# Two orders for the first eight chunks of a down projection whose left operand is still being made

## The chip, the cores and the metric

The kernel runs on one core of a Trainium2 chip. The metric is the device time of one execution in microseconds, as the median of three runs. A profile of one further execution, with a time stamp for each instruction, gives the trace.

## The reference

Two transformer blocks on 256 rows of width 2048, in float32. The first has a gated linear attention, then an MLP; the second is a hybrid block. The change concerns the MLP of the first block alone:

```python
def _sq_relu_mlp(h, w_up, w_down):      # w_up 2048 x 8192, w_down 8192 x 2048
    a = jax.nn.relu(h @ w_up)
    return (a * a) @ w_down
# in first_block:
h = h + _sq_relu_mlp(_rmsnorm(h, mlp_norm[i]), mlp_w_up[i], mlp_w_down[i])
```

## The kernel before

**Chunks.** All weight matrices are laid out by the host in one stream of chunks, each 128 x 2048 floats (1 MB): four k tiles of 128 by a column block of 512. SyncE loads them in program order into a ring of four slots (`w_raw`), each when the chunk four before has been used. Each float32 value is split in a high part, rounded to the fp32r format (`w_hi`, ScalarE, L1137), and a low part, the rest (`w_lo`, VectorE, L1810, in the same memory as `w_raw`). TensorE multiplies high by high, low by high and high by low (L585, L586, L587), so a chunk is 4 k tiles x 2 halves of the rows x 3 = 24 matmuls of 512 columns. ScalarE and VectorE work three chunks ahead of TensorE (`AHEAD = 3`). The count `lo_ready` tells TensorE that a chunk is split.

**The MLP.** It runs in four groups (`part` or `g`), each over 2048 of the 8192 hidden columns: 19 chunks of up projection (column blocks 0 to 3; blocks 2 and 3 and some products of sums are formed by `up_pair`) and then 16 chunks of down projection. The down projection sums over k, here the group's 2048 hidden columns, in four quarters q; quarter q is what up block q gave, after relu, square and a transposition. Its column blocks b are those of the result. A down chunk is a pair (b, q). I call the down chunks d0 to d15 in the order in which they come; in the loops over `c` they are c = 19 to 34.

**How a quarter becomes ready.** VectorE or ScalarE takes the up block out of PSUM into `nat`. VectorE transposes it within 32 x 32 squares (`turned`, L2076 for quarters 2 and 3). ScalarE squares it while it moves the squares to their places (`sq`, L1330, sixteen activations in two lots of eight) and rounds it to `a_hi` (L1334). VectorE forms `a_lo` (L2080) and counts `a_low`; TensorE waits for that count before the chunk that uses the quarter first.

**Order on the engines.** Nothing schedules at run time: each engine has one queue, in the order in which the loops write it. In VectorE's loop step c the additions and transpositions stand ahead of `split(c + 3)`. For up block 3 the step is c = 19: the addition L2071 reads its PSUM half and frees it, then comes quarter 2's `a_lo`, then the split of chunk 22.

**PSUM.** The accumulators are two halves, `acc[:, blk % 2]`. Every column block of every product takes the next number `blk`, so a new block needs the half of the block two before, and waits for it in its first matmul:

```python
if first and blk >= 2:
    accs.wait(pe, blk - 2)
```

Down block 0 takes the half of up block 2, down block 1 that of up block 3. The order of the first eight down chunks interleaves two column blocks, and comes from a function:

```python
def LATER(blocks):
    return [(0, 0), (0, 1), (0, 2), (1, 0), (1, 1), (1, 2), (0, 3), (1, 3)] + [(b, q) for b in range(2, blocks) for q in range(4)]
```

Of the kernel before, what the change touches and what calls it, by code (L numbers as in the profile page):

```python
# [17 lines left out]
def build(nc, x, x_turned, mem, mem_turned, stream, cols, rows, wglow, wab, wgu, shapes, masks, out):  # L18
# [27 lines left out]
    with ExitStack() as ctx:  # L46
# [517 lines left out]
        def _(pe):  # L564
            def chunk(c, lhs, k0, blk, first, last, n_k=4, width=N, rows_=(0, 1), done=True, second_half=None):

                if c >= EARLY:
                    pe.wait_ge(lo_ready, ready(c))
                if first and blk >= 2:

                    accs.wait(pe, blk - 2)
                wh = w_hi[:, c % SLOTS].rearrange("p (k n) -> p k n", n=width)
                wl = low_part(c).rearrange("p (k n) -> p k n", n=width)
                for k in range(n_k):
                    if second_half and k == n_k // 2:
                        second_half()
                    if c < EARLY:
                        pe.wait_ge(lo_ready, ready(c, k))
                    if c < NB:
                        pe.wait_ge(x0_low, 4 * c + k + 1)  # L580
                    for m in rows_:
                        xh = lhs[0][:, k0 + k, m * P:(m + 1) * P]
                        xl = lhs[1][:, k0 + k, m * P:(m + 1) * P]
                        dst = acc[:, blk % 2, m, 0:width]
                        pe.matmul(dst, xh, wh[:, k], start=first and k == 0, stop=False)  # L585
                        pe.matmul(dst, xh, wl[:, k], start=False, stop=False)  # L586
                        mm = pe.matmul(dst, xl, wh[:, k], start=False, stop=last and k == n_k - 1)  # L587
                if done:
                    mm.then_inc(used, 1)
                return mm  # L590
# [108 lines left out]
            for c in range(48):  # L699
                b, q = divmod(c, 4)  # L700
# [13 lines left out]
            for c in range(16):  # L714
                b, q = LATER(4)[c]
# [16 lines left out]
            def up_pair(g):  # L732

                c0, left, right = C_MLP + GROUP * g, accs.name["up", g, 2], accs.name["up", g, 3]
                chain, both = tpf(0)[:, 0:N], tpf(0)[:, N:2 * N]

                def of_x(q, m):
                    return [t[:, 4 * q:4 * q + 4, m * P:(m + 1) * P] for t in X]

                def of_s(n):  # L740
                    return s_hi[:, n], s_lo[:, n]

                if g == 0:
                    tps.wait(pe, tps.name["s", 3])
                    tps.wait(pe, tps.name["o", 3])
                else:
                    pe.wait_ge(pair_out, pair_step(g - 1, "p7"))
                product(c0 + 8, *of_x(0, 0), chain, start=True, stop=True)
                chunk(c0 + 9, X, 8, left, True, False)
                if g == 0:  # L750
                    pe.wait_ge(s_formed, 2)
                accs.wait(pe, right - 2)
                product(c0 + 10, *of_s(3), acc[:, right % 2, 0], start=True)
                chunk(c0 + 11, X, 12, left, False, True)
                product(c0 + 12, *of_s(0), both, start=True, stop=True)
                pe.wait_ge(pair_out, pair_step(g, "p1"))
                product(c0 + 13, *of_s(1), chain, stop=True)
                product(c0 + 14, *of_x(1, 0), acc[:, left % 2, 0], stop=True)
                pe.wait_ge(pair_out, pair_step(g, "p6"))
                product(c0 + 15, *of_s(2), chain, stop=True)  # L760
                product(c0 + 16, *of_x(1, 1), acc[:, left % 2, 1], stop=True)
                chunk(c0 + 17, X, 8, right, False, False, rows_=(0,), done=False)
                chunk(c0 + 17, X, 8, right, True, False, rows_=(1,))
                chunk(c0 + 18, X, 12, right, False, True)

            for g in range(GROUPS):
                for c in range(8):
                    b, q = divmod(c, 4)
                    if g == 0 and c < 4:
                        pe.wait_ge(b_low, ROUNDED["norm1", c] + 1)  # L770
                    chunk(C_MLP + GROUP * g + c, X, 4 * q, accs.name["up", g, b], q == 0, q == 3)
                up_pair(g)
                for c in range(16):
                    b, q = LATER(4)[c]
                    if b == 0:
                        pe.wait_ge(a_low, 4 * g + q + 1)
                    chunk(C_MLP + GROUP * g + 19 + c, A, 4 * q, accs.name["down", g, b], q == 0, q == 3)
# [231 lines left out]
            for c in range(50):  # L1009
                if c < 48:  # L1010
                    b, q = divmod(c, 4)
# [8 lines left out]
            for nb in range(NB):  # L1020
                for j in range(16):
                    c = 50 + 16 * nb + j
                    br, q, k0 = BRANCH[j]
# [12 lines left out]
            for c in range(16):  # L1036
                b, q = divmod(c, 4)
# [25 lines left out]
            for c in range(12):  # L1063
                b, q = divmod(c, 4)
# [10 lines left out]
            g = tps.name["xo_"]  # L1075
# [17 lines left out]
            for g in range(2):  # L1093
                for c in range(48):
                    b, q = divmod(c, 4)
                    if c >= 32:
                        b, q = 8 + LATER(4)[c - 32][0], LATER(4)[c - 32][1]
# [699 lines left out]
        def _(dve):  # L1797
# [624 lines left out]
            for nb in range(NB):  # L2422
                for j in range(16):
                    c = 50 + 16 * nb + j
                    br, _, _ = BRANCH[j]
                    if j in (4, 14, 15):

                        gk = 3 * nb + {4: 0, 14: 2, 15: 1}[j]
                        gate, blk = accs.name[("gate", nb, br)], accs.name[("br", nb, br)]
                        dve.wait_ge(used, C_2 + c + 1)  # L2430
                        accs.wait(dve, gate)
                        t = nat[:, gk % 2]
                        dve.scalar_tensor_tensor(mg[nb % 2][:] if br == "sb" else t, t, 1.0, acc[:, blk % 2], ALU.add, ALU.mult).then_inc(accs.sem(blk), 1)
                        accs.wait(dve, blk)
                        if br == "dn":
                            dve.tensor_tensor(mg[nb % 2][:], mg[nb % 2][:], t, ALU.add).then_inc(mg_ready, 1)
                        if br == "swa":
                            dve.wait_ge(mg_ready, 2 * nb + 1)
                            dve.tensor_tensor(mg[nb % 2][:], mg[nb % 2][:], t, ALU.add).then_inc(mg_ready, 1)
                            dve.wait_ge(mg_ready, 2 * nb + 2)  # L2440
                            if nb:
                                dve.wait_ge(b_moved, SIDE["merged", nb - 1] + 1)
                            dve.transpose(mturned[:], mg[nb % 2][:].rearrange("p m n -> p (m n)")).then_inc(b_turned, 1)
                            if nb == 3:
                                half_carried(("merged", 3), mm[:], mturned[:])
                    if nb == 0:
                        attention_side(c)
                    elif j == 2:
                        merged_low(nb - 1)
                    split(C_2 + c + AHEAD)  # L2450
                    sliding_sums(c)
# [166 lines left out]
def LATER(blocks):  # L2618

    return [(0, 0), (0, 1), (0, 2), (1, 0), (1, 1), (1, 2), (0, 3), (1, 3)] + [(b, q) for b in range(2, blocks) for q in range(4)]  # L2620


def _stream(parts):

    out = []
    for w, width, *last_later in parts:
        k, n = w.shape
        kt = k // P
        per = CH // width

        a = w.reshape(kt // per, per, P, n // width, width).transpose(3, 0, 2, 1, 4)
        a = a.reshape(-1, P, CH)
        if last_later:
            a = a[[4 * b + q for b, q in LATER(a.shape[0] // 4)]]
        out.append(a)
    return np.concatenate(out, 0)

# [93 lines left out]
```

## Time and profile before

| | |
|---|---|
| median of 3 runs | 2502.48 us (2501.55 to 2504.41) |
| profiled execution | 2504.08 us, of it span 2502.2 us |
| TensorE (PE) matmuls busy | 2474.4 us |
| VectorE (DVE) busy | 1585.0 us |
| ScalarE (ACT) busy | 1586.5 us |
| mean granted TensorE clock | 0.996 of full |

A matmul's record lasts 0.39 us, but the next starts 0.23 us after it, so the busy time is that of the union. PEld is TensorE's loading of weights into the array, which goes on beside matmuls. The granted clock is a share of the full 2.4 GHz; 0.5 is 1.2 GHz. The times of the timelines are microseconds from the start of the span.

### The profile page before, as it was taken

What the parts mean: (1) busy time and instruction counts of PE and PEld (TensorE: products, weight loads), DVE (VectorE), ACT (ScalarE), POOL (GpSimd) and SP (SyncE); (2) the same over time, 40 slices, a digit from 0 to 9 for tenths busy, and PEclk for the clock granted to TensorE, in tenths of its full rate; (3) what the DMA queues carried; (4) which work ended last, traced back from release to release, by engine and by line L of the source; (5) the groups of instructions that cost most, each with busy time, mean ns of one, the idle gap of its engine ahead of it and who ended that gap; (6) DMA issues with size and microseconds to landing.
All of it is one profiled execution on the core that took longest, in us unless ns stands there. A gap on an engine that the chain in (4) does not pass through costs nothing.

```text
span 2502.2 us, 29766 instructions
## 1 busy us (share of the span) xinstructions
PE 2474.4 (99%) x12403; PEld 2041.9 (82%) x12403; DVE 1585.0 (63%) x1314; ACT 1586.5 (63%) x2107; POOL 33.4 (1%) x41
## 2 busy tenths in 40 slices
PE   9999999999999999999999999999999999999998
PEld 7887788788788788788888888888888888888887
DVE  5775559657547547567765685445666676646675
ACT  6635778736737637886465585545597688638873
POOL 0000000000000000000000000000000000000000
PEclk9999999999999999999999999999999999999999
DMA  8554456455464465455444445555655455555554
GB/s 285 188 199 168 170 191 235 149 199 208 154 233 168 168 231 185 173 185 185 155 158 147 152 177 184 195 192 195 259 195 184 177 196 191 196 190 197 191 196 152
DMA packets 69367, 472.37 MB, mean 189 GB/s; under 512 B 7913, under 2 KB 8353, under 8 KB 13425
## 3 DMA queue, kind: packets, MB, share of 16 engines
q1 hardware_dynamic: 67040, 460.62, 50.7%
q0 software_dynamic: 1312, 7.73, 0.8%
q8 instruction: 98, 1.61, 0.3%
q10 hardware_dynamic: 880, 2.11, 0.2%
q14 instruction: 37, 0.30, 0.0%
HBM read 468.33 MB, written 2.11 MB: 188 GB/s over the span
## 4 chain that ended last, share of the span: by engine, by line
PE 90%; ACT 5%; issue 2%; DVE 2%; DMA 0%; SPq 0%; POOLq 0%; POOL 0%; DVEq 0%; ACTq 0%
PE acc L585 28%; PE acc L586 28%; PE acc L587 28%; ACT sq L1330 2%; ACT w_hi L1137 2%; PE tp L918 0%; DVE w_lo L1810 0%; PE tp L729 0%; PE tp L728 0%; PE tp L727 0%; PE tp L851 0%; PE tp L605 0%; DVE turned L2076 0%; PE acc L727 0%; PE acc L729 0%
## 5 line engine op out<-in xcount | busy, mean ns | idle before, releaser
L1810 DVE TENSOR_TENSOR w_lo<-w_raw,w_hi 128x2048 fp32r<-128x2048 f32 x422 | 964.8, 2289 | 703.4 <-ACT w_hi L1137 700.9
L1137 ACT ACTIVATE w_hi<-w_raw 128x2048 fp32r<-128x2048 f32 x422 | 806.6, 1915 | 442.4 <-DMA w_raw<-in_stream 433.2
L585 PE MATMUL acc<-w_hi,x_hi 128*128 128x512 f32 (+1 forms) x2112 | 826.4, 391 | 1.0 <-DVE w_lo L1817 0.4
L587 PE MATMUL acc<-w_hi,x_lo 128*128 128x512 f32 (+1 forms) x2112 | 819.8, 388 | 0.0
L586 PE MATMUL acc<-w_lo,x_hi 128*128 128x512 f32 (+1 forms) x2112 | 819.6, 388 | 0.0
L585 PEld LDWEIGHTS acc<-w_hi,x_hi 128*128 128x128 f32 x2112 | 396.9, 188 | 86.1 <-issue 2.5
L587 PEld LDWEIGHTS acc<-w_hi,x_lo 128*128 128x128 f32 x2112 | 396.9, 188 | 81.2
L586 PEld LDWEIGHTS acc<-w_lo,x_hi 128*128 128x128 f32 x2112 | 397.1, 188 | 80.0 <-issue 1.0
L585 PE MATMUL acc<-w_hi,a_hi 128*128 128x512 f32 x1120 | 440.3, 393 | 16.6 <-DVE a_lo L2080 14.3
L586 PE MATMUL acc<-w_lo,a_hi 128*128 128x512 f32 x1120 | 438.3, 391 | 0.0
L587 PE MATMUL acc<-w_hi,a_lo 128*128 128x512 f32 x1120 | 438.2, 391 | 0.0
L585 PEld LDWEIGHTS acc<-w_hi,a_hi 128*128 128x128 f32 x1120 | 211.7, 189 | 64.7 <-DVE a_lo L2080 16.0
L587 PEld LDWEIGHTS acc<-w_hi,a_lo 128*128 128x128 f32 x1120 | 211.6, 189 | 44.0
L586 PEld LDWEIGHTS acc<-w_lo,a_hi 128*128 128x128 f32 x1120 | 211.7, 189 | 43.3
L1330 ACT ACTIVATE sq<-turned 32x256 f32<-32x256 f32 x256 | 106.2, 415 | 27.3 <-DVE turned L2076 23.8
L1724 ACT ACTIVATE fm<-fturned 32x256 f32<-32x256 f32 x256 | 106.2, 415 | 4.2 <-DVE fturned L2561 1.2
L1154 ACT ACTIVATE nat<-acc,rstd 128x512 f32<-128x512 f32 (+1 forms) x80 | 50.0, 677 | 79.4 <-PE acc L587 78.3
L1886 DVE TENSOR_TENSOR h<-acc,h 128x1024 f32<-128x1024 f32 x35 | 42.8, 1223 | 46.4 <-PE acc L587 46.4
L1154 ACT ACTIVATE nat<-acc,rhalf 128x512 f32<-128x512 f32 x36 | 22.8, 684 | 66.3 <-PE acc L587 66.2
L1176 ACT ACTIVATE sq<-turned 32x256 f32<-32x256 f32 x112 | 46.5, 415 | 10.8 <-DVE turned L1853 9.5
L585 PE MATMUL acc<-w_hi,m_hi 128*128 128x512 f32 x128 | 50.0, 390 | 0.0
L586 PE MATMUL acc<-w_lo,m_hi 128*128 128x512 f32 x128 | 49.9, 390 | 0.0
(436 smaller groups left out, 1679.3 us busy)
## 6 DMA issues: line engine op xcount, KB each, us to landing
w_raw<-in_stream SPq DMA_DIRECT2D x422, 1024.0 KB, 4.8
w_raw<-in_stream SPq DMA_DIRECT2D x16, 256.0 KB, 7.8
raw_T<-in_stream SPq DMA_DIRECT2D x4, 1024.0 KB, 6.9
raw_b<-in_stream SPq DMA_DIRECT2D x4, 1024.0 KB, 8.9
h<-in_x SPq DMA_DIRECT2D x4, 512.0 KB, 14.7
frow<-in_rows POOLq DMA_DIRECT2D x2, 1024.0 KB, 6.2
m_raw<-in_mem_turned POOLq DMA_DIRECT2D x1, 2048.0 KB, 9.7
memt<-in_mem POOLq DMA_DIRECT2D x1, 2048.0 KB, 11.9
```

Source lines behind the costliest of these rows:

```text
L585: pe.matmul(dst, xh, wh[:, k], start=first and k == 0, stop=False)
L586: pe.matmul(dst, xh, wl[:, k], start=False, stop=False)
L587: mm = pe.matmul(dst, xl, wh[:, k], start=False, stop=last and k == n_k - 1)
L1137: act.activation(w_hi[:, c % SLOTS], raw(c), ACT.Copy).then_inc(hi_ready, 1)
L1154: ins = act.activation(dst[:, m], src[:, m], func, scale=scales[:, j, m:m + 1])
L1176: ins = act.activation(dst[32 * to:32 * to + 32, :, :, q], src[32 * q:32 * q + 32, :, :, to], ACT.Copy, scale=scale)
L1330: ins = act.activation(dst[32 * to:32 * to + 32, :, :, q], src[32 * q:32 * q + 32, :, :, to], ACT.Square)
L1724: ins = act.activation(dst[32 * to:32 * to + 32, :, :, q], src[32 * q:32 * q + 32, :, :, to], ACT.Copy)
L1810: dve.tensor_tensor(low_part(c), raw(c), w_hi[:, c % SLOTS].bitcast(F32), ALU.subtract).then_inc(lo_ready, 1)
L1886: dve.tensor_tensor(hn, acc[:, blk % 2], hn, ALU.add).then_inc(accs.sem(blk), 1)
```

## The change

The down chunks of the first block's MLP take another order, `TURNS`, in TensorE's loop and in the host's layout of the stream. The two other products that use `LATER` keep it.

```diff
-                    b, q = LATER(4)[c]
+                    b, q = TURNS(4)[c]
                     if b == 0:
                         pe.wait_ge(a_low, 4 * g + q + 1)
                     chunk(C_MLP + GROUP * g + 19 + c, A, 4 * q, accs.name["down", g, b], q == 0, q == 3)
...
+def TURNS(blocks):
+
+    return [(b, q) for q in range(4) for b in range(2)] + [(b, q) for b in range(2, blocks) for q in range(4)]
...
-    for w, width, *last_later in parts:
+    for w, width, *order in parts:
...
-        if last_later:
-            a = a[[4 * b + q for b, q in LATER(a.shape[0] // 4)]]
+        if order:
+            a = a[[4 * b + q for b, q in order[0](a.shape[0] // 4)]]
...
-        parts += [(up[:, 2048 * g:2048 * (g + 1)], 512), (down[2048 * g:2048 * (g + 1)], 512, "last later")]
+        parts += [(up[:, 2048 * g:2048 * (g + 1)], 512), (down[2048 * g:2048 * (g + 1)], 512, TURNS)]
```

As pairs (b, q), d0 to d7 were (0,0) (0,1) (0,2) (1,0) (1,1) (1,2) (0,3) (1,3) and are now (0,0) (1,0) (0,1) (1,1) (0,2) (1,2) (0,3) (1,3).

TensorE's queue in group 0, the first matmul of each of d0 to d6, with the semaphores that it waits for (`acc_took_dve0` and `acc_took_dve1` are counts of VectorE's releases of the two PSUM halves; 23 matmuls without a wait lie between two of these rows). Before:

```order
L585 MATMUL acc<-w_hi,a_hi 128x512 [waits acc_took_dve0,lo_ready,a_low]
...
L585 MATMUL acc<-w_hi,a_hi 128x512 [waits lo_ready,a_low]
...
L585 MATMUL acc<-w_hi,a_hi 128x512 [waits lo_ready,a_low]
...
L585 MATMUL acc<-w_hi,a_hi 128x512 [waits acc_took_dve1,lo_ready]
...
L585 MATMUL acc<-w_hi,a_hi 128x512 [waits lo_ready]
...
L585 MATMUL acc<-w_hi,a_hi 128x512 [waits lo_ready]
...
L585 MATMUL acc<-w_hi,a_hi 128x512 [waits lo_ready,a_low]
```

Now, the same seven places:

```order
L585 MATMUL acc<-w_hi,a_hi 128x512 [waits acc_took_dve0,lo_ready,a_low]
...
L585 MATMUL acc<-w_hi,a_hi 128x512 [waits acc_took_dve1,lo_ready]
...
L585 MATMUL acc<-w_hi,a_hi 128x512 [waits lo_ready,a_low]
...
L585 MATMUL acc<-w_hi,a_hi 128x512 [waits lo_ready]
...
L585 MATMUL acc<-w_hi,a_hi 128x512 [waits lo_ready,a_low]
...
L585 MATMUL acc<-w_hi,a_hi 128x512 [waits lo_ready]
...
L585 MATMUL acc<-w_hi,a_hi 128x512 [waits lo_ready,a_low]
```

The wait for the third quarter has moved from d2 to d4, and the wait for the second PSUM half from d3 to d1.

VectorE's queue in group 0, from the second addition for up block 2 to the `a_lo` of the last quarter, is the same before and now (the two numbers after `turned` and `sq` are those of their two buffers; the two L1810 ahead of the first L2076 and of L2071 split chunks d1 and d2):

```order
L2067 TENSOR_TENSOR nat<-nat,tp 128x1024
L1810 TENSOR_TENSOR w_lo<-w_raw,w_hi 128x2048 [waits hi_ready,dve_step]
L2076 STREAM_TRANSPOSE turned_116<-nat 128x1024 [waits sq_moved,pair_out]
L1810 TENSOR_TENSOR w_lo<-w_raw,w_hi 128x2048 [waits hi_ready]
L2071 TENSOR_TENSOR nat<-nat,acc 128x1024 [waits used]
L2080 TENSOR_TENSOR a_lo<-sq_118,a_hi 128x1024 [waits a_high]
L1810 TENSOR_TENSOR w_lo<-w_raw,w_hi 128x2048 [waits hi_ready]
L2076 STREAM_TRANSPOSE turned_117<-nat 128x1024 [waits sq_moved,pair_out]
L1810 TENSOR_TENSOR w_lo<-w_raw,w_hi 128x2048 [waits hi_ready] x2
L2080 TENSOR_TENSOR a_lo<-sq_119,a_hi 128x1024 [waits a_high]
```

Nothing moved here: L2071, which releases the second PSUM half, stands behind the split of d2 in both kernels.

## Rows read from the trace of the kernel before

**Rows 1.** The page, part 1: busy us (share of the span) and instructions
```profile
PE 2474.4 (99%) x12403; PEld 2041.9 (82%) x12403; DVE 1585.0 (63%) x1314; ACT 1586.5 (63%) x2107; POOL 33.4 (1%) x41
```

**Rows 2.** Waits of PE: waiting line, releaser, total us, times, longest us
```profile
PE acc L585 <- DVE a_lo L2080: 14.3, 4, 3.8
PE acc L585 <- DVE w_lo L1810: 2.5, 5, 0.6
```

**Rows 3.** Timeline of PE, group 0: start, duration, instruction [idle before]
```profile
464.70 0.39 PE L585 MATMUL acc<-w_hi,a_hi 128*128 128x512 f32 x1
...
475.35 0.39 PE L587 MATMUL acc<-w_hi,a_lo 128*128 128x512 f32 x1
479.22 0.50 PE L585 MATMUL acc<-w_hi,a_hi 128*128 128x512 f32 x1 [3.48 <-DVE a_lo L2080]
...
490.95 0.51 PE L585 MATMUL acc<-w_hi,a_hi 128*128 128x512 f32 x1 [0.56 <-DVE w_lo L1810]
...
497.27 0.50 PE L585 MATMUL acc<-w_hi,a_hi 128*128 128x512 f32 x1 [0.54 <-DVE w_lo L1810]
...
502.84 0.39 PE L585 MATMUL acc<-w_hi,a_hi 128*128 128x512 f32 x1
```

**Rows 4.** Timeline of DVE, group 0
```profile
473.44 2.29 DVE L1810 TENSOR_TENSOR w_lo<-w_raw,w_hi 128x2048 fp32r<-128x2048 f32 x1 [5.41 <-ACT w_hi L1137]
475.65 1.21 DVE L2071 TENSOR_TENSOR nat<-nat,acc 128x1024 f32<-128x1024 f32 x1
477.94 1.23 DVE L2080 TENSOR_TENSOR a_lo<-sq,a_hi 128x1024 fp32r<-128x1024 f32 x1 [1.08 <-ACT a_hi L1334]
...
488.61 2.29 DVE L1810 TENSOR_TENSOR w_lo<-w_raw,w_hi 128x2048 fp32r<-128x2048 f32 x1 [5.41 <-ACT w_hi L1137]
494.92 2.29 DVE L1810 TENSOR_TENSOR w_lo<-w_raw,w_hi 128x2048 fp32r<-128x2048 f32 x1 [4.02 <-ACT w_hi L1137]
```

**Rows 5.** Timeline of ACT, group 0
```profile
468.06 3.41 ACT L1330 ACTIVATE sq<-turned 32x256 f32<-32x256 f32 x8 [3.58 <-DVE turned L2076]
471.49 1.92 ACT L1137 ACTIVATE w_hi<-w_raw 128x2048 fp32r<-128x2048 f32 x1
...
492.99 5.51 ACT L1137 ACTIVATE w_hi<-w_raw 128x2048 fp32r<-128x2048 f32 x3
```

**Rows 6.** Timeline of PE, groups 1 and 2, and the first of group 3
```profile
641.56 0.39 PE L585 MATMUL acc<-w_hi,a_hi 128*128 128x512 f32 x1
...
656.09 0.79 PE L585 MATMUL acc<-w_hi,a_hi 128*128 128x512 f32 x1 [3.48 <-DVE a_lo L2080]
...
661.79 0.40 PE L586 MATMUL acc<-w_lo,a_hi 128*128 128x512 f32 x1
...
819.34 0.39 PE L585 MATMUL acc<-w_hi,a_hi 128*128 128x512 f32 x1
...
834.21 0.80 PE L585 MATMUL acc<-w_hi,a_hi 128*128 128x512 f32 x1 [3.83 <-DVE a_lo L2080]
...
839.40 0.39 PE L585 MATMUL acc<-w_hi,a_hi 128*128 128x512 f32 x1
...
997.21 0.39 PE L585 MATMUL acc<-w_hi,a_hi 128*128 128x512 f32 x1
```

**Rows 7.** Windows: stretch, us, busy by engine, PEclk, DMA share, GB/s
```profile
655.00:662.00 7.00, 5.92 (x14) 4.64 (x15) 4.48 (x3) 4.67 (x8) 0.00 (x0) 0.52 0.25 105
832.80:839.40 6.60, 5.19 (x13) 4.14 (x14) 4.67 (x3) 4.29 (x7) 0.00 (x0) 0.51 0.26 112
```

**Rows 8.** Timeline of DVE, L2071 in groups 1, 2 and 3
```profile
652.51 1.21 DVE L2071 TENSOR_TENSOR nat<-nat,acc 128x1024 f32<-128x1024 f32 x1
...
830.63 1.21 DVE L2071 TENSOR_TENSOR nat<-nat,acc 128x1024 f32<-128x1024 f32 x1
...
1008.16 1.22 DVE L2071 TENSOR_TENSOR nat<-nat,acc 128x1024 f32<-128x1024 f32 x1
```

**Rows 9.** The page, part 6: DMA issue, times, KB each, median us to landing
```profile
w_raw<-in_stream SPq DMA_DIRECT2D x422, 1024.0 KB, 4.8
```

More of the change, by code:

```diff
@@ L2678 @@
     up, down = a["mlp_w_up"][0], a["mlp_w_down"][0]
-    parts = [(w1[:, :6144], 512), (a["gla_w_out"][0], 512, "last later")]
+    parts = [(w1[:, :6144], 512), (a["gla_w_out"][0], 512, LATER)]
     for g in range(4):
-        parts += [(up[:, 2048 * g:2048 * (g + 1)], 512), (down[2048 * g:2048 * (g + 1)], 512, "last later")]
+        parts += [(up[:, 2048 * g:2048 * (g + 1)], 512), (down[2048 * g:2048 * (g + 1)], 512, TURNS)]
     w2 = a["w_in_2"][0]
@@ L2701 @@
             parts += [(up2[:, c:c + 512], 512), (up2[:, 4096 + c:4096 + c + 512], 512)]
-        parts += [(down2[2048 * g:2048 * (g + 1)], 512, "last later")]
+        parts += [(down2[2048 * g:2048 * (g + 1)], 512, LATER)]
     stream = _stream(parts)
```

## The prediction

> **What bounds the kernel now.** I read the page first: TensorE is busy for 2474.4 of 2502.2 us [rows 1], so the time moves only where TensorE issues nothing or issues slowly. The chain of waits of TensorE names where it stands still: 14.3 us in four waits on `a_lo`, the longest 3.8, and 2.5 us in five on `w_lo` [rows 2]. All else is under 1.3 us a line. The four waits are the four groups of the MLP, at the third chunk of the down projection. I call the down chunks d0, d1, ... and then read group 0 from the timelines of the three engines.
>
> TensorE [rows 3]: d0 starts at 464.70, and 47 matmuls later the last of d1 starts at 475.35, so one matmul is 0.2266 us and a chunk of 24 is 5.44. Unstalled, d1 starts at 470.14, d2 at 475.58 and d6 at 464.70 + 6 x 5.443 = 497.36. In fact d2 starts at 479.22 (3.64 late), d4 waits for 0.56 and d5 for 0.54, and d6 starts at 502.84. The price of group 0 up to d6 is 5.48 us. The engine's own idle column says 3.48 + 0.56 + 0.54 because it counts from the end of a 0.39 us matmul; I use starts.
>
> Who is waited for: VectorE is one queue in program order [rows 4]. It turns up block 2, stands for 5.41 us until ScalarE has rounded chunk d2 (473.44), then adds the fourth up block (L2071, 475.65, done 476.86), then makes the third quarter's `a_lo` (477.94 to 479.17), which releases d2 0.05 us later. ScalarE, in front of it, is nearly without a gap [rows 5]: it moves squares from 468.06 and rounds d2's weights at 471.49 to 473.41.
>
> **The clock.** Groups 1 and 2 cost more than group 0, and not by a longer wait alone. In group 1 the matmul after the stall starts at 656.09 and the fourteenth at 661.79: 5.70 us for 13 steps that take 2.95, so 2.75 lost [rows 6]. The clock of 655 to 662 is 0.52 of full [rows 7], that is some 6.7 us at 1.2 instead of 2.4 GHz. Group 2 is alike: twelve steps in 5.19 us instead of 2.72 (2.47 lost), at 0.51. Counted back from 661.8, the clock of group 1 fell at 655.1, some 2.4 us after the last matmul ended (due start of d2 less one step plus 0.39, 652.6). Groups 0 and 3, with a stall of 3.5 us too, kept full clock.
>
> Price of each group up to d6: group 0, 5.48; group 1, d2 is due at 641.56 + 10.89 = 652.45 and starts at 656.09, so 3.64 + 2.75 = 6.39, and no later wait; group 2, due at 830.23 and starts at 834.21, 3.98 + 2.47 = 6.45. Group 3's stall is what the four leave, 14.3 - 3.48 - 3.48 - 3.83 = 3.5, and the rest of the `w_lo` waits is there too, so 5.5 like group 0 [rows 2, 3, 6]. Sum **23.8 us**.
>
> **The change, part by part.** The number of matmuls, transfers and roundings is the same; weight chunks of the stream change places with equal ones, 1 MB each. What the eight first chunks wait for changes.
>
> Taken away: the wait for the third quarter of `a_lo` moves from d2 to d4. d4 starts at 493 or later, `a_lo` is there at 479.17. All 23.8 us above go, if nothing replaces them: the `w_lo` waits of d4 and d5 end at fixed times, 490.90 and 497.21 [rows 4].
>
> Added: the second column block now opens at d1, not d3, and opening it needs the PSUM half that L2071 frees. In group 0 d1 is due at 470.14 and L2071 ends at 476.86. With 0.05 of release d1 starts at 476.91, **6.77 us late**. Behind it on TensorE stands everything. Does L2071 move? What it stands behind (d2's rounding, and the squares before it) depends on the up projection alone, not on d0 or d1, and VectorE's row is unchanged. In the other groups L2071 starts at 652.51, 830.63 and 1008.16 [rows 8] and takes 1.21; d1 is due at 641.56 + 5.44 = 647.00, 824.78 and 997.21 + 5.44 = 1002.65. Late by 6.77, 7.11 and 6.77. Sum **27.4 us**.
>
> Then the clock. TensorE will idle from 470.3 (end of d0's last matmul) to 476.9, 6.6 us, in each of four groups. No gap that long stands in the trace; the nearest rows are the gaps of 3.5 and 3.8 that lost the clock in two of four cases, 2.4 us in. A gap of 6.6 should lose it every time. Price for each: the rows say 2.75 and 2.47. Bounds: a fall 2.4 us into the gap comes 4.2 before the restart, which leaves 2.5 us of a 6.7 us stretch at half clock, 1.25 lost; a fall just before the restart leaves all of it, 3.35. I take 2.4, between the middle of the bounds (2.3) and the rows' mean (2.6): **9.6 us** in all, bounds 5.0 and 13.4.
>
> The Trainium skill, "TensorE: Matmul & The Clock Gate", section "HAM oscillation — how this bites in real kernels", says that idle gaps between bursts throttle the array again, so that each burst starts cold, and speaks against any longer gap. By that rule the stalls to come cost the 9.6 us beside their own length; by a reading in which the clock stays, as in groups 0 and 3, they cost only their length. This trace bears it out in two stalls of four.
>
> What lies after d1, in group 0: d1 ends at 476.91 + 5.44 + 2.4 = 484.8, and d2 to d6 start at 484.8, 490.2, 495.6, 501.1 and 506.5. They need `w_lo` of d4 by 495.6 (there at 490.90), of d5 by 501.1 (497.21), and the fourth quarter of `a_lo`, whose VectorE place is right behind d5's (497.21 + 1.23 = 498.4). The ring has four slots: d5's load waits for d1, now until 484.8; a load lands in 4.8 us [rows 9], at 489.6, and ScalarE comes to it at 492.99 [rows 5]. 3.4 us of cover; without it ScalarE would slip by what exceeds it, and d5 has 3.9 more. So nothing else waits up to d6, and from there TensorE is alone at the front. The new wait replaces the old ones.
>
> Sum: + 27.4 + 9.6 - 23.8 = **+13.2 us**. On the profiled execution's 2504.08 that is 2517.3; on the median, 2502.48, it is 2515.7. The profiled one lies 1.6 above the median, which may be its two clock losses (1.9 together over group 0's price). I forecast 2516.5, slower by 0.56%.
>
> **Rivals.** (a) *The clock stays.* Each restart then costs 0.13 as at d4 in group 0, and the sum is 27.4 + 0.5 - 23.8 = +4.1, 2506.6 on the median, within 0.2%. For it: two stalls of 3.5 us kept the clock. Against: two did not, and the new gap goes 4.2 us beyond the point where it fell. 6 in 100. If it stays in two groups of four, 2511.
>
> (b) *The second block's PSUM half is free in time, and the change doesn't cost.* Its place is L2071, whose operands are ready as soon as the up projection ends: if it ran while VectorE stands between 468.0 and 473.4, d1 would wait for nothing. The gain would still not be 23.8 us. d5 cannot start before its `w_lo` at 497.26, so d6 starts at 502.8, as now: the ScalarE and VectorE queue takes the place of the `a_lo` wait. Nothing in groups 0 and 3, at most the 0.9 and 1.0 of lost clock in 1 and 2: 2500.6 to 2502.5. It decides where d1's wait with its clock loss is under 5.5 us, that is where L2071 ended before 473.5. Program order puts it behind the rounding of d2, so 3 in 100. This also bounds any gain at 1.9 us.
>
> (c) *More is late behind the stall.* Loads that now start later meet ScalarE's busy stretch: beyond the 3.4 + 3.9 us of cover each us costs one, four times; with 1.5 us each, 2522. 4 in 100, since a load would have to take over 12 us.
>
> **How the numbers follow.** The forecast case has 86 in 100; its own range, from the bounds of the clock's price and the two bases (2502.48 + 8.6; 2504.08 + 17.0), is 2511 to 2521. (a) has 6, (b) 3, (c) 4, something unseen 1. The range 2510.5 to 2521 leaves out (a), (b), (c) and the tails, some 2 in 10. A difference below 0.2%, 5 us, can't be told from none here. Slower by over 0.2% is the forecast, (c) and half of (a): 0.9; the same 0.08; faster 0.02.
>
> **What would show it.** TensorE's waits: no `a_lo` any more, and four waits on `nat` L2071 of about 6.6 us (6.9 in group 2); no `w_lo` waits at d4 and d5; after each stall some ten matmuls at 0.43 instead of 0.23 us, and a half clock before it. VectorE's L2071 as far behind d0 as now, 12.2 us. Wrong: a clock that stays whole in the gaps, a shorter wait at d1, or new waits on `w_lo` behind it.

## The result

The changed kernel takes 2515.81 us (median of 4 runs, 2515.35 to 2516.9) against 2502.5 (4 runs, 2501.55 to 2504.41): ratio 1.0053, 95% interval 1.0035 to 1.007. It is slower by 13.3 us. The profiled executions are 2515.97 and 2504.08 us, spans 2514.1 and 2502.2.

The page of the changed kernel, part 1, answers to [rows 1]. TensorE does the same 12403 matmuls in nearly the same busy time (2474.4 us before) and its share falls:

```profile
PE 2475.1 (98%) x12403; PEld 2042.7 (81%) x12403; DVE 1585.2 (63%) x1314; ACT 1587.1 (63%) x2107; POOL 33.4 (1%) x41
```

TensorE's waits, to be held against [rows 2]. The waits on `a_lo` are gone and those on `w_lo` L1810 nearly; one releaser that was not in the list before stands at its head, four times:

```profile
PE acc L585 <- DVE nat L2071: 27.1, 4, 7.1
...
PE acc L585 <- DVE w_lo L1810: 0.3, 1, 0.3
```

TensorE's timeline in group 0, around the opening of d1. The last matmul of d0 starts at 469.89, d1 at 476.96; the steps behind it are 0.57 us, five times 0.43 and once 0.40, and from 480.06 on 0.23 again:

```profile
469.89 0.39 PE L587 MATMUL acc<-w_hi,a_lo 128*128 128x512 f32 x1
476.96 0.76 PE L585 MATMUL acc<-w_hi,a_hi 128*128 128x512 f32 x1 [6.69 <-DVE nat L2071]
477.53 0.63 PE L586 MATMUL acc<-w_lo,a_hi 128*128 128x512 f32 x1
...
480.06 0.39 PE L586 MATMUL acc<-w_lo,a_hi 128*128 128x512 f32 x1
```

VectorE in the same stretch answers to [rows 4], every start within 0.06 us of what it was: L2071 did not move, TensorE came to ask for it earlier.

```profile
473.39 2.29 DVE L1810 TENSOR_TENSOR w_lo<-w_raw,w_hi 128x2048 fp32r<-128x2048 f32 x1 [5.39 <-ACT w_hi L1137]
475.60 1.21 DVE L2071 TENSOR_TENSOR nat<-nat,acc 128x1024 f32<-128x1024 f32 x1
477.89 1.23 DVE L2080 TENSOR_TENSOR a_lo<-sq,a_hi 128x1024 fp32r<-128x1024 f32 x1 [1.07 <-ACT a_hi L1334]
```

The granted clock (the number before the last two) answers to [rows 7]. It is whole when TensorE has just stopped and half before TensorE starts again, and it stays half until 480.0. The last two lines are the same for group 3, where the last matmul of d0 ends at 1011.08 and d1 starts at 1017.77: there the clock fell later, 4.8 us into the gap instead of 2.9:

```profile
470.00:473.00 3.00, 0.28 (x2) 0.00 (x0) 0.00 (x0) 2.95 (x5) 0.00 (x0) 1.00 0.48 161
474.00:475.00 1.00, 0.00 (x0) 0.00 (x0) 1.00 (x1) 0.98 (x3) 0.00 (x0) 0.50 0.36 148
478.00:480.00 2.00, 2.00 (x6) 1.60 (x5) 1.43 (x2) 2.00 (x2) 0.00 (x0) 0.50 0.00 0
480.00:482.00 2.00, 2.00 (x10) 1.62 (x9) 2.00 (x2) 0.89 (x2) 0.00 (x0) 1.00 0.00 0
...
1011.10:1015.90 4.80, 0.00 (x0) 0.00 (x0) 1.70 (x1) 4.69 (x9) 0.00 (x0) 1.00 0.58 220
1016.00:1022.70 6.70, 4.93 (x12) 3.89 (x13) 5.05 (x4) 5.62 (x8) 0.00 (x0) 0.50 0.00 0
```

One number compares all kernels below: the **loss** of a group, which is the start of d7 less the start of d0 less 7 x 5.443 us, read from TensorE's timeline. It holds the stalls and the slow matmuls behind them. The losses are those of the profiled execution of each kernel, the medians those of all its executions. Groups 0 to 3:

| kernel | losses, us | sum | median, us (kernel before, same chip) |
|---|---|---|---|
| before | 5.5, 6.4, 6.5, 5.5 | 23.9 | 2502.5 |
| changed | 8.4, 9.0, 9.4, 9.3 | 35.9 | 2515.8 (2502.5) |
| e1 | 5.5, 7.4, 6.6, 6.3 | 25.8 | 2505.2 (2503.0) |
| e2 | 6.2, 6.2, 6.6, 6.2 | 25.3 | 2505.6 (2503.0) |
| e3 | 7.0, 7.0, 7.3, 7.0 | 28.2 | 2508.2 (2503.0) |
| e4 | 6.6, 6.4, 6.5, 5.5 | 24.9 | 2503.4 (2503.0) |
| f1 | 8.8, 9.1, 9.3, 9.4 | 36.6 | 2516.4 (2503.3) |
| f2 | 1.7, 1.7, 1.7, 1.7 | 6.9 | 2486.4 (2503.3) |
| f3 | 0.4, 0.4, 0.4, 0.4 | 1.6 | 2481.4 (2503.3) |
| f4 | 2.6, 2.6, 2.6, 2.6 | 10.4 | 2492.1 (2503.3) |

The losses of the two kernels of the case differ by 12.1 us, their profiled executions by 11.9: these four places hold the whole difference.

### The profile page after: what moved, and what is told of

Its sections match the earlier page's. It is cut to its first block, busy times and chain, and to the rows that moved or that the text cites. A ratio compares the mean times of both kernels' runs of the same rounds, so it can differ in the third digit from the quotient of the medians.

```text
span 2514.1 us, 29766 instructions
## 1 busy us (share of the span) xinstructions
PE 2475.1 (98%) x12403; PEld 2042.7 (81%) x12403; DVE 1585.2 (63%) x1314; ACT 1587.1 (63%) x2107; POOL 33.4 (1%) x41
## 4 chain that ended last, share of the span: by engine, by line
PE 92%; ACT 3%; DVE 2%; issue 2%; DMA 0%; SPq 0%; POOLq 0%; POOL 0%; DVEq 0%; ACTq 0%
PE acc L585 29%; PE acc L586 29%; PE acc L587 29%; ACT w_hi L1137 1%; ACT sq L1330 1%; DVE w_lo L1810 1%; PE tp L918 0%; PE tp L728 0%; PE tp L729 0%; PE tp L727 0%; PE tp L851 0%; PE tp L605 0%; PE acc L727 0%; PE acc L729 0%; PE acc L728 0%
## 5 line engine op out<-in xcount | busy, mean ns | idle before, releaser
L1810 DVE TENSOR_TENSOR w_lo<-w_raw,w_hi 128x2048 fp32r<-128x2048 f32 x422 | 965.0, 2289 | 717.3 <-ACT w_hi L1137 714.9
L585 PE MATMUL acc<-w_hi,x_hi 128*128 128x512 f32 (+1 forms) x2112 | 825.0, 391 | 1.6 <-DVE w_lo L1817 1.0
L586 PE MATMUL acc<-w_lo,x_hi 128*128 128x512 f32 (+1 forms) x2112 | 818.6, 388 | 0.0
L585 PE MATMUL acc<-w_hi,a_hi 128*128 128x512 f32 x1120 | 440.4, 393 | 27.3 <-DVE nat L2071 27.1
L585 PEld LDWEIGHTS acc<-w_hi,x_hi 128*128 128x128 f32 x2112 | 396.5, 188 | 86.4 <-issue 2.5
L586 PEld LDWEIGHTS acc<-w_lo,x_hi 128*128 128x128 f32 x2112 | 396.7, 188 | 80.2 <-issue 1.0
L586 PE MATMUL acc<-w_lo,a_hi 128*128 128x512 f32 x1120 | 438.7, 392 | 0.0
L585 PEld LDWEIGHTS acc<-w_hi,a_hi 128*128 128x128 f32 x1120 | 212.2, 190 | 73.8 <-issue 29.3
L586 PEld LDWEIGHTS acc<-w_lo,a_hi 128*128 128x128 f32 x1120 | 212.4, 190 | 44.0
L1330 ACT ACTIVATE sq<-turned 32x256 f32<-32x256 f32 x256 | 106.1, 415 | 27.3 <-DVE turned L2076 23.8
L585 PE MATMUL acc<-w_hi,m_hi 128*128 128x512 f32 x128 | 49.9, 390 | 0.0
L586 PE MATMUL acc<-w_lo,m_hi 128*128 128x512 f32 x128 | 49.8, 389 | 0.0
```

The lines of the kernel that those rows point to most:

```text
L1330: ins = act.activation(dst[32 * to:32 * to + 32, :, :, q], src[32 * q:32 * q + 32, :, :, to], ACT.Square)
L1810: dve.tensor_tensor(low_part(c), raw(c), w_hi[:, c % SLOTS].bitcast(F32), ALU.subtract).then_inc(lo_ready, 1)
```

## Experiments

The kernel before ran beside each of them. The medians of e1 to e4 are of 11 executions (the kernel before: 33), those of f1 to f4 of 5 (9). A ratio is that of the kernel to the kernel before, with its 95% interval.

**e1: the PSUM half is released before d2's split.** In VectorE's loop:

```diff
-                    if c == 19:
+                    if c == 18:
                         blk = accs.name["up", part, 3]
                         dve.wait_ge(used, C_MLP + GROUP * part + 19)
                         dve.tensor_tensor(nat[:, 1], nat[:, 1], acc[:, blk % 2], ALU.add).then_inc(accs.sem(blk), 1)
```

(and the block now stands behind the transposition of step 18, ahead of the split.)

> The changed kernel (2515.8 us) with one VectorE addition moved: L2071, which frees the second PSUM half, stands one loop step earlier, ahead of the split of d2 instead of behind it. Theory: the new wait is that release, late only by its place in VectorE's queue. Then in group 0 it runs at 468.0 to 469.2, d1 starts on time at 470.1 and the 6.8 us stalls with their clock loss are gone. But d4 and d5 cannot start before their w_lo at 490.9 and 497.2, which ScalarE's queue sets, so d6 starts at 502.8 as in the kernel before: 2500.5 to 2503.5 us, with waits on w_lo of about 0.7, 3.2 and 0.7 us a group in place of those on L2071. Rival A: the waits themselves were the price, and with both gone the whole 24 us come back: about 2480. Rival B: the release is late for another cause than its place: 2515 as now.

2505.24 us, ratio 1.0009 (1.0 to 1.0018). Of the 13.3 us over the kernel before 2.2 are left, at the edge of what can be told from none; the other 11 hang on the place of one addition. The theory's waits are there, and rivals A and B are out. TensorE's waits, then its timeline at d3, d4 and d5 of group 0 and at d4 of group 1:

```profile
PE acc L585 <- DVE w_lo L1810: 16.2, 11, 3.2
```

```profile
481.72 0.50 PE L585 MATMUL acc<-w_hi,a_hi 128*128 128x512 f32 x1 [0.54 <-DVE w_lo L1810]
...
490.66 0.47 PE L585 MATMUL acc<-w_hi,a_hi 128*128 128x512 f32 x1 [3.20 <-DVE w_lo L1810]
...
496.87 0.50 PE L585 MATMUL acc<-w_hi,a_hi 128*128 128x512 f32 x1 [0.53 <-DVE w_lo L1810]
...
667.56 0.77 PE L585 MATMUL acc<-w_hi,a_hi 128*128 128x512 f32 x1 [3.17 <-DVE w_lo L1810]
```

The median lies 1.7 us above the range given. The losses say why. In group 0 the clock stayed whole through d4's wait of 3.2 us and the loss is the 5.5 us of the kernel before, as expected. In groups 1 to 3 it fell, and the 24 matmuls of d4 took 2.9, 1.7 and 1.7 us more than 5.44; of that only d5's short wait could absorb some.

**e2: the second block opens at d2.** `TURNS` begins `[(0, 0), (0, 1), (1, 0), (0, 2), (1, 1), (1, 2), (0, 3), (1, 3)]`, in the loop and in the stream alike.

> The changed kernel with another order, (0,0) (0,1) (1,0) (0,2) (1,1) (1,2) (0,3) (1,3): the second block opens at d2 and the third quarter comes at d3; VectorE and ScalarE untouched. Theory (ScalarE's chain sets d4 and d5): d2 is due at 475.6 and finds the PSUM half at 476.9, 1.3 us late, no clock loss; d3 starts at 482.5, d4 waits some 3 us for its w_lo at 490.9, d5 0.6 at 497.2, d6 starts at 502.8 as before the change: 2500.5 to 2503 us. Rival A (a wait costs its own length): the 14 us of a_lo waits are saved but for 1.3 us a group: about 2493. Rival C (a reader of the prediction's sum without the chain): slower than before by the new wait, 2505 or more.

2505.57 us, ratio 1.0008 (1.0 to 1.0017). Rival A's gain of 10 us is out, so removing the `a_lo` wait doesn't bring d4 forward: it still stands until its split. But the theory's figure is 2.6 us too low, and rival C's sentence ("2505 or more") fits the number, though not its reason: the new wait is short, as expected (1.27), and d4 waits 2.78. What was not expected is the clock. TensorE, group 0, then three stretches around d4:

```profile
476.59 0.47 PE L585 MATMUL acc<-w_hi,a_hi 128*128 128x512 f32 x1 [1.27 <-DVE nat L2071]
...
490.54 0.50 PE L585 MATMUL acc<-w_hi,a_hi 128*128 128x512 f32 x1 [2.78 <-DVE w_lo L1810]
```

```profile
487.80:491.70 3.90, 1.16 (x5) 0.99 (x6) 2.29 (x1) 3.76 (x10) 0.00 (x0) 1.00 0.74 252
491.80:495.10 3.30, 3.30 (x9) 2.62 (x8) 0.61 (x1) 3.30 (x3) 0.00 (x0) 0.50 0.02 5
495.20:500.00 4.80, 4.80 (x22) 3.94 (x21) 4.80 (x3) 2.86 (x2) 0.00 (x0) 1.00 0.19 44
```

Behind a gap of only 2.8 us the clock fell in all four groups, and not in the gap: in group 0 five matmuls of d4 still run at the full rate, and the fall comes 1.2 us after TensorE has started again. The half clock lasts 3.4 us here, not 6.8, and d4's 24 matmuls take 1.8 us more than 5.44 in each group. That the idling before d4 caused it is concluded from e3 below; no run kept TensorE busy in this order.

**e3: TensorE is kept busy inside the wait.** In TensorE's loop of the changed kernel:

```diff
                     b, q = TURNS(4)[c]
+                    if c == 1:
+                        for _ in range(26):
+                            pe.matmul(tp[:, 1].rearrange("p k t -> p (k t)")[:, 0:N], x_hi[:, 0, 0:P], x_hi[:, 0:2].rearrange("p k t -> p (k t)"), start=True, stop=True)
```

> The changed kernel with 26 extra matmuls (512 columns, into a PSUM bank that nothing else uses in the MLP, from x_hi) between d0 and d1 of each group, about 5.9 us of work inside the wait of 6.8 us. Their result is not used. Theory: the slow matmuls behind each stall are the clock, lost because TensorE idled; kept busy it stays at 2.4 GHz, and the 8.2 us go, less 0.13 of restart a group: 2508 us, granted clock 1.00 over the groups. Rival D: the slow matmuls come from what ScalarE, VectorE or the loads do at that moment, and stay: 2515.8. Rival E: the extra matmuls also delay d1 (they last longer than the wait, or loads and splits are slowed by them): over 2516.

2508.18 us, ratio 1.0021 (1.0012 to 1.003): 5.1 us over the kernel before where the changed kernel has 13.3, for 104 matmuls more. The theory's 2508 is met: the losses fall by 7.8 us, the medians by 7.6. The filler in group 0 and the wait behind it, then the clock of both sides:

```profile
469.65 6.05 PE L777 MATMUL tp<-x_hi 128*128 128x512 f32 x26
476.52 0.47 PE L585 MATMUL acc<-w_hi,a_hi 128*128 128x512 f32 x1 [0.81 <-DVE nat L2074]
```

```profile
465.00:476.00 11.00, 10.70 (x48) 8.53 (x46) 5.59 (x4) 8.23 (x17) 0.00 (x0) 1.00 0.53 191
476.00:490.00 14.00, 13.48 (x60) 11.19 (x61) 6.93 (x5) 11.52 (x19) 0.00 (x0) 1.00 0.29 97
```

(Lines of this kernel are numbered three higher: L2074 is L2071.) d1 still starts 6.87 us late, and not one matmul behind it is slow. The slow matmuls were the clock, and the clock was lost by idling: rival D is out.

**e4: the early release in the kernel before.** The same move of L2071, nothing else.

> The kernel before (2502.5 us) with the same early place of L2071 alone. In its order the second block opens at d3, 484.8, when the half has been free for 8 us, so nothing waits for L2071. Theory: same, 2501.5 to 2503.5, with the same a_lo waits of 3.5 us and w_lo waits of 0.5. Rival: the addition's 1.2 us taken out from ahead of the third quarter's a_lo brings that a_lo forward and shortens the 3.5 us wait: up to 1.1 us a group, 2498; against it stands VectorE's 1.08 us of waiting for a_hi right there.

2503.44 us, ratio 1.0 (0.9991 to 1.0009). No difference, as expected: its waits on `a_lo` are the old 14.3 us in four.

```profile
PE acc L585 <- DVE a_lo L2080: 14.3, 4, 3.8
```

So the early release by itself is worth nothing; it is worth some 11 us where the order needs it. In this profile three groups lost the clock instead of two, and the sum of losses is 1.0 higher for that alone.

**f1: VectorE takes half of the squares of quarters 2 and 3.** The changed kernel with:

```diff
+                    if c in (18, 20):
+                        n = 2 + (c - 18) // 2
+                        dve.wait_ge(nat_turned, 4 * part + n + 1)
...
+                        for q in (2, 3):
+                            for to in range(4):
+                                own = src[32 * q:32 * q + 32, :, :, to]
+                                ins = dve.tensor_tensor(dst[32 * to:32 * to + 32, :, :, q], own, own, ALU.mult)
+                        ins.then_inc(half_squared, 1)
```

ScalarE leaves its second lot out for these two quarters and waits for `half_squared` before it rounds.

> The changed kernel with ScalarE's queue relieved: of the sixteen squarings that move quarters 2 and 3 into place, VectorE does eight (squared by itself as a product), in the stretches in which it stands idle, so ScalarE has 3.4 us less ahead of each rounding. L2071 keeps its place behind the split of d2, and d2's rounding stands ahead of ScalarE's second lot, so it isn't brought forward. Theory: d1 waits for L2071 as long as now, 6.8 us with clock loss, and what becomes faster behind it was hidden there already: 2515 to 2516.5, as the changed kernel. Rival: ScalarE's chain as a whole is the bound, so the changed kernel gains too, 2505 or less.

2516.44 us, ratio 1.0052 (1.0039 to 1.0064), and the wait for the release is what it was (in this kernel L2076 is the release and L586 the old L585):

```profile
PE acc L586 <- DVE nat L2076: 26.8, 4, 6.7
```

Relieving ScalarE is worth nothing while d1 waits for a release that it doesn't bring forward. The rival, 2505 or less, is out.

**f2: both, the early release and the shared squares,** in the changed order.

> The changed order, L2071 early as in the first experiment, and the squares shared with VectorE. Theory: with both the PSUM half and ScalarE's chain out of the way the order shows its own worth. In group 0 d1 starts on time, d2's w_lo is there about on time, d4's w_lo at some 488 against a due 486.7 (1.3 us), d5 on time: loss of under 2 us a group where the kernel before has about 5.7. 2486 to 2490. Rival A: only d4 and d5's waits shift, because VectorE's added squares (8 x 0.3 to 0.4 us, twice a group) delay its splits by as much as ScalarE gains: 2500 and more.

2486.43 us, ratio 0.9932 (0.992 to 0.9945), near the lower end of the range; rival A is out. The loss that is left is 1.7 us a group: 1.2 at d4, which waits for its `w_lo` (L1815 here), 0.3 at d2 for the same reason, and 0.1 of restart behind each:

```profile
PE acc L586 <- DVE w_lo L1815: 4.4, 5, 1.0
```

**f3 and f4: the fourth block's chain starts earlier,** in the changed and in the old order. Both hold the two edits of f2 as well. In VectorE's loop, against f2:

```diff
-                    if c in (18, 20):
-                        n = 2 + (c - 18) // 2
+                    if c in (18, 19):
+                        n = 2 + (c - 18)
                         dve.wait_ge(pair_out, pair_step(part, f"up{n}"))
```

with ScalarE's `pair_scaled(part, 3)` ahead of its split in step 19. VectorE's transposition of block 3 now stands ahead of the third quarter's `a_lo`. f4 differs from f3 in the order of the eight chunks and in nothing else.

> As the kernel before this one, and the fourth up block's scaling (ScalarE) and transposition (VectorE) stand ahead of the rounding of d3 and of the third quarter's a_lo: the fourth quarter's chain starts some 3.5 us earlier and the third quarter's a_lo comes 1.2 us later, at about 478.1. In the changed order that a_lo is needed at d4, 486.4, so the delay is free, and d4's w_lo is in time. Theory: no wait over 0.5 us in the down projection, loss under 1 us a group: 2480 to 2484. Rival: the split of d3, now behind both, becomes late (due 480.9): 1 us a group more.

> Exactly the same instructions as the run before this one, in the order of the kernel before: (0,0) (0,1) (0,2) (1,0) ... Theory: now the order decides. The third quarter's a_lo is needed at d2, 475.6, and comes at 478.1: 2.5 us a group, with some clock loss: 2489 to 2494, 8 us or more above the same kernel in the changed order. Rival: the order is worth nothing here either (as between the kernel before and the first experiment): within 2 us of it.

f3: 2481.4 us, ratio 0.9912 (0.9899 to 0.9926). f4: 2492.13 us, ratio 0.9953 (0.994 to 0.9965). Both lie in their ranges and both rivals are out. The order that cost 13 us in the case is worth 10.7 here. The losses of the two profiled executions show 8.8 of it. The rest is not in f4's profile: that execution and one more took 2490.3 us at a mean granted clock of 0.999, the three others 2492.1 to 2493.0 at 0.998, which points to a lost clock in them; no trace of those is kept. VectorE in f3 (the line numbers are shifted: L2077 is the transposition, L2081 the release, L2090 the shared squares, L2095 `a_lo`):

```profile
467.59 1.18 DVE L2081 TENSOR_TENSOR nat<-nat,acc 128x1024 f32<-128x1024 f32 x1
468.80 3.44 DVE L2090 TENSOR_TENSOR sq<-turned 32x256 f32<-32x256 f32 x8
473.08 2.29 DVE L1815 TENSOR_TENSOR w_lo<-w_raw,w_hi 128x2048 fp32r<-128x2048 f32 x1 [0.85 <-ACT w_hi L1138]
475.29 1.24 DVE L2077 STREAM_TRANSPOSE turned<-nat 128x1024 f32<-128x1024 f32 x1
476.45 1.18 DVE L2095 TENSOR_TENSOR a_lo<-sq,a_hi 128x1024 fp32r<-128x1024 f32 x1
```

The release is done at 468.77, ahead of d1's due time (464.33 + 5.44 = 469.77). `a_lo` is done at 477.6, which is 2.4 us too late for d2 (475.2) and 8.5 too early for d4 (486.1). The 5.4 us in which VectorE stood idle ahead of d2's split [rows 4] are filled but for 0.9. TensorE's waits in f4, and the first of them:

```profile
PE acc L586 <- DVE a_lo L2095: 9.3, 4, 2.3
```

```profile
478.15 0.50 PE L586 MATMUL acc<-w_hi,a_hi 128*128 128x512 f32 x1 [2.33 <-DVE a_lo L2095]
```

## Why the prediction was right, point by point

**The new wait.** Forecast 6.77, 6.77, 7.11 and 6.77 us, 27.4 in all, at d1 on L2071. Measured from start to start: 6.84, 6.86, 7.22 and 6.85, 27.8 in all. The difference is mostly the release: in group 0 0.15 us from the end of L2071 (476.81) to d1's start, where `a_lo` had shown 0.05. e1 shows by removal that the wait is L2071's place in VectorE's queue.

**The clock.** Forecast lost in every group, 2.4 us each, 9.6 in all, bounds 5.0 and 13.4. Lost in every group, 1.5, 2.1, 2.2 and 2.4 (loss less stall), 8.2 in all. The term was mis-sized by 1.4 us, inside its bounds. The way in which the bounds were worked out holds: a stretch at half clock of the same length in every group, 6.8 us here and 6.7 forecast, of which only what lies behind the restart costs. It fell 2.9, 4.1, 4.7 and 4.8 us after the last matmul had ended, so 3.1, 4.2, 4.4 and 5.0 us of it lay behind the restart, and half of that is the price. Where in its bounds the fall would come was a guess: the forecast's 2.4 us means 4.7 us into the gap, which groups 2 and 3 show and groups 0 and 1 don't. e3 shows that it is the clock and that TensorE kept busy doesn't lose it. That the clock stays, rival (a), is out. The Trainium skill ("TensorE: Matmul & The Clock Gate", section "HAM oscillation — how this bites in real kernels") says that the array is throttled again in a long idle gap between bursts and the next burst starts cold. The four gaps of 6.7 to 7.1 us agree: d1 began at half clock each time.

**What goes.** All 23.8 us of [rows 2, 3, 6] went: no `a_lo` wait, no `w_lo` wait at d4 or d5, every chunk from d2 to d7 in 5.44 us. The cover for the loads held, so rival (c) is out too.

**The sum.** Forecast +13.2; the losses say +12.1, the profiled executions +11.9, the medians +13.3. The terms were 0.4 too low for the stalls and 1.4 too high for the clock, and these errors partly cancel. The medians agree with the forecast better than the terms do, partly by chance: the executions of the kernel before spread over 2501.6 to 2505.2 us (33 runs beside e1 to e4), and those with the highest times, 2504.8 and more, have the lowest granted clock, 0.994. The profiled one lay in the upper part.

**Rival (b), an early release.** It was worked out as a gain of at most 1.9 us, because ScalarE's and VectorE's chain sets d4 and d5. e1 is that rival, made: 2.2 us slower than before, where 2500.6 to 2502.5 us was forecast. The bound on the gain held, and group 0 came out as worked out (loss 5.5 us). Groups 1 to 3 did not, since the wait moved to d4 in one piece of 3.2 us and the clock was lost around it. In the changed order e1, f1 and f2 show two bounds, one behind the other: the release moved alone removes the wait at d1 and leaves the chain's (2505.2), the shared squares alone gain nothing (2516.4), both together gain (2486.4). How much of f2's gain the old order would have had with the same two edits is not shown; only with the third edit were both orders run (f3 and f4), and there the old order too gained 11 us over the kernel before.

**What had been overlooked.** Rival (b), and the expectations of e1 and e2 after it, left the clock out of the wait that appears at d4. It was lost around that wait in three groups of e1 (3.2 us) and in all four of e2 (2.8 us), and both kernels came out some 2 us above their figure. The prediction also reads the clock as something that falls in a gap; in all groups of e2 and in two of e1 it fell after TensorE had started again.

## What to carry to other kernels

When an operand is late, moving its first use back asks for everything else that the new order needs earlier: here a PSUM half, needed at d1 instead of d3. For each moved chunk list all that its first instruction waits for, and put beside it when that is ready in the old trace.

If a stall goes, work out what the same place would wait for next before counting a gain; behind TensorE's 5.5 us a group stood the chain of ScalarE and VectorE, which let d5 start no earlier. An order can be right and still lose until the queue that feeds it is put in the same order: this one lost 13 us, and gained 11 once the release, the squares and the transposition stood where it wanted them.

## What the runs showed of the hardware

The length of an idle gap alone doesn't say whether TensorE's clock falls. In the profiled executions it fell around 8 of 8 gaps of 6.7 to 7.1 us (changed, f1), 2 of 2 of 3.8 (before, e4), 3 of 6 of 3.5 (before, e4), 3 of 4 of 3.2 (e1) and 4 of 4 of 2.8 (e2), and around none of the four of 2.3 (f4) nor any shorter one. What decides between equal gaps is open.

Read from the granted clock of ever narrower stretches, the fall came 2.0 to 5.1 us after the last matmul had ended. In 14 cases that was inside the gap; the clock then stayed at half for 6.8 us, and the chunk behind the gap took 1.5 to 3.0 us longer. In six (e2, and groups 2 and 3 of e1) it was 0.5 to 1.2 us after TensorE had started again; the half clock lasted 3.4 us and the chunk took 1.7 to 1.8 us longer. These prices hold the 0.1 us that a restart costs at full clock too (e3).

A product on VectorE over 32 partitions x 256 took 0.42 us, as long as ScalarE's square of the same piece (0.415); in f1 to f4 eight squares of each of the quarters 2 and 3 went from one engine to the other. In f1, which differs from the changed kernel in nothing else, that cost nothing that can be seen: 13.1 us over the kernel before, as against 13.3.
